# Taking feeds, a first turn and a turn order over into a 1-core RWKV, GLA and short-convolution kernel, with modulation pieces and back-end orders dealt anew

## The reference, cut to what matters

```python
def rwkv7_scan(r, decay, k, v, kk, b, reverse):
    def step(S, inp):
        r_t, w_t, k_t, v_t, kk_t, b_t = inp
        sa = jnp.einsum('bhij,bhj->bhi', S, -kk_t)
        S = (S * w_t[:, :, None, :] + sa[..., None] * b_t[:, :, None, :]
             + v_t[..., None] * k_t[:, :, None, :])
        return S, jnp.einsum('bhij,bhj->bhi', S, r_t)
...
def first_block(x, p, ...):
        z = rms_norm(h, norm_mix_pre[i]) @ w_in[i]
        y = concatenate([rwkv7_mixer(z_rwkv), gla_mixer(z_gla)]) @ w_out[i]
        h = h + rms_norm(y, norm_mix_post[i])
        hn = rms_norm(h, norm_ffn_pre[i])
        f = (silu(hn @ ffn_gate[i]) * (hn @ ffn_up[i])) @ ffn_down[i]
        h = h + rms_norm(f, norm_ffn_post[i])
        e = p[i] @ ple_proj[i]
        gate = jax.nn.sigmoid(h @ ple_gate[i] + ple_gate_b[i])
        h = h + rms_norm(gate * e, norm_ple[i])
...
def second_block(x, c, ada_w, ada_b, ...):
        mod = silu(c) @ ada_w[i] + ada_b[i]
        sh_m, sc_m, g_m, sh_f, sc_f, g_f = jnp.split(mod, 6, axis=-1)
        # modulated norm, short convolution mixer, gated residual; the same around a SwiGLU
```

## Time and the profile before

| | us |
|---|---|
| median of three runs (3123.69 to 3125.21) | 3123.69 |
| profiled execution | 3124.51 |
| its span in the trace | 3122.7 |
| TensorE busy with matmuls | 2912.3 (93%) |
| VectorE busy | 1467.9 (47%) |
| ScalarE busy | 1150.3 (37%) |
| GpSimd busy | 280.8 (9%) |
| stretch from 1044 us on, TensorE busy | 2045 of 2079 |

### The profile page before, as it was taken

How to read it: one execution, slowest core, us unless ns; L and a number is a source line. 1 busy time by engine, 2 the same in 40 slices (tenths; PEclk the granted TensorE clock), 3 DMA queues, 4 the chain that set the end, 5 groups by cost and what they waited for, 6 DMA issues and landing times.

```text
span 3122.7 us, 56580 instructions
## 1 busy us (share of the span) xinstructions
PE 2912.3 (93%) x25024; PEld 2370.8 (76%) x25024; DVE 1467.9 (47%) x2047; ACT 1150.3 (37%) x1891; POOL 280.8 (9%) x318
## 2 busy tenths in 40 slices
PE   6986799688887799999999999999999999999997
PEld 5765666587785488888888887788887888888886
DVE  3668676245454454433343326666436533234323
ACT  5665565222223243322332225533234333242322
POOL 1000023444441100000000000000000000000000
PEclk8987899799998799999999999999999999999998
DMA  4320244311100123222222222222222222223222
...
DMA packets 99541, 273.07 MB, mean 87 GB/s; under 512 B 8224, under 2 KB 35488, under 8 KB 99296
## 3 DMA queue, kind: packets, MB, share of 16 engines
...
## 4 chain that ended last, share of the span: by engine, by line
PE 63%; DVE 2%; ACT 1%; issue 0%; DMA 0%; DVEq 0%; ACTq 0%
PE be_ps L2937 47%; PE be_ps L2958 15%; PE be_ps L2971 1%; DVE be_ring L2719 0%; PE be_ps L2664 0%; PE be_ps L2658 0%; DVE be_total L2677 0%; ACT be_whi L3004 0%; DVE be_raw_r L3111 0%; DVE big L2691 0%; DVE big L2701 0%; ACT big L3010 0%; DMA be_raw<-in_ple_gate 0%; DVE big_r L2729 0%; DVE ext_r L2729 0%
## 5 line engine op out<-in xcount | busy, mean ns | idle before, releaser
L3111 DVE TENSOR_TENSOR be_raw_r<-be_raw,be_whi 128x1024 fp32r<-128x1024 f32 x361 | 442.2, 1225 | 997.3 <-ACT be_whi L3004 996.9
L2937 PE MATMUL be_ps<-ext_r,be_whi 128*128 128x512 f32 x2304 | 714.9, 392 | 13.0 <-PEq L2331 8.6
L3004 ACT CAST be_whi<-be_raw 128x1024 fp32r<-128x1024 f32 x361 | 378.8, 1049 | 898.6 <-DMA be_raw<-in_ffn_down 317.2
L2937 PE MATMUL be_ps<-big_r,be_whi 128*128 128x512 f32 x2048 | 642.2, 394 | 0.8 <-DVE be_raw_r L3111 0.5
L2937 PEld LDWEIGHTS be_ps<-ext_r,be_whi 128*128 128x128 f32 x2304 | 432.9, 189 | 106.5 <-issue 10.6
L2937 PEld LDWEIGHTS be_ps<-big_r,be_whi 128*128 128x128 f32 x2048 | 383.0, 188 | 95.9 <-DVE big_r L2727 1.0
L2937 PE MATMUL be_ps<-ext_r,be_raw_r 128*128 128x512 f32 x1152 | 449.8, 390 | 0.0
L2937 PE MATMUL be_ps<-big_r,be_raw_r 128*128 128x512 f32 x1024 | 408.1, 398 | 0.0
L2958 PE MATMUL be_ps<-ext_r,be_whi 128*128 128x512 f32 x1152 | 354.9, 389 | 0.0
L2937 PEld LDWEIGHTS be_ps<-ext_r,be_raw_r 128*128 128x128 f32 x1152 | 217.1, 188 | 45.5
L2958 PEld LDWEIGHTS be_ps<-ext_r,be_whi 128*128 128x128 f32 x1152 | 216.2, 188 | 45.1
...
## 6 DMA issues: line engine op xcount, KB each, us to landing
be_raw<-in_ffn_gate SPq DMA_DIRECT2D x88, 512.0 KB, 3.5
be_raw<-in_ffn_up SPq DMA_DIRECT2D x88, 512.0 KB, 3.5
be_raw<-in_ffn_down SPq DMA_DIRECT2D x88, 512.0 KB, 3.5
be_raw<-in_conv_in SPq DMA_DIRECT2D x48, 512.0 KB, 3.4
gp_ada<-in_ada POOLq DMA_DIRECT2D x24, 512.0 KB, 3.7
rp_ada<-in_ada POOLq DMA_DIRECT2D x24, 512.0 KB, 3.8
rwkv_prepared<-big SPq DMA_DIRECT2D x16, 512.0 KB, 3.2
be_raw<-in_w_out SPq DMA_DIRECT2D x16, 512.0 KB, 3.5
```

The costliest lines, as they stand in the source:

```text
L2937: mm = pe.matmul(ps[:, bank], part[:, k * P:(k + 1) * P], xs(k), start=(k == 0 and i == 0), stop=(k == KD - 1 and i == 2))
L3004: act.copy(w.hi[:, n % 3], w.raw[:, n % 3]).then_inc(w.hi_ready, 1)
L3111: dve.tensor_tensor(w.lo(n), w.raw[:, n % 3], w.hi[:, n % 3].bitcast(F32), ALU.subtract).then_inc(w.lo_ready, 1)
```

## The change

- **GLA projection.** The pieces per step become 3,3,2,2,2,2,2,3,0,0,3,2 instead of 3,3,2,2,2,2,2,2,0,0,3,3, and the last tile's side products come after its 48 matmuls.
- **RWKV projection.** In step 8 VectorE's reciprocal comes ahead of `accumulate(3)`. SP issues the first four feeds of the mixing at the end of the stage and waits for them. ScalarE ends with a dummy Exp.
- **Mixing, opening.** No feeds for turns 0 and 1; VectorE makes the first alpha and rho in place of GpSimd; the four first score groups get banks 0, 4, 6 and 2 and stand in a row.
- **Mixing, turns.** TensorE's `front_nv(t + 1)` follows `products(0)` instead of `products(1)`; ScalarE's copy of nv comes after both copies of u. A turn's feed is six DMAs of 128 KB instead of two of 384 KB, each waiting for TensorE's marks of four turns before.
- **Back end.** In stage "eg" the groups of steps 2 and 3 take banks 0, 2, 3, 1; norm pieces beside the projections and the last gate are placed at other positions.

The diff, cut to its core:

```diff
@@ -613,7 +613,7 @@
         a_up = sb("aup", [P, 2 * P])
-        modulation = Modulation(core, ctx, "gp", dram_ada, c, mod, 0, (3, 3, 2, 2, 2, 2, 2, 2, 0, 0, 3, 3))
+        modulation = Modulation(core, ctx, "gp", dram_ada, c, mod, 0, (3, 3, 2, 2, 2, 2, 2, 3, 0, 0, 3, 2))
         acc = ctx.enter_context(nc.psum_tensor("gp_acc", [P, 2, T], F32))
@@ -792,7 +792,7 @@
                 for k in range(KD):
-                    if k >= 5 and k - 5 < len(side_products):
+                    if s < n_tiles - 1 and k >= 5 and k - 5 < len(side_products):
                         modulation.product(pe, side_products[k - 5])
@@ -804,6 +804,9 @@
                     decay_sum(n)
+                if s == n_tiles - 1:
+                    for n in side_products:
+                        modulation.product(pe, n)
@@ -1161,6 +1164,22 @@
+def turn_tokens(d, j):
+    n = j if d == 0 else NBLK - 1 - j
+    return slice(n * BLK, (n + 1) * BLK)
...
+def fed_pair(pieces):
+    return pieces.rearrange("p (s d k t) -> p s d k t", s=2, d=2, k=6)
...
+def first_fed(z):
+    return fed_pair(z[:, 12:15].rearrange("p a t -> p (a t)"))
@@ -1185,7 +1204,7 @@
         sem = lambda name: core.sem(f"rp_{name}")
-        first_hi = sem("first_hi")
+        first_hi, fed_early, exp_table = sem("first_hi"), sem("fed_early"), sem("exp_table")
         filled, edged, summed, mixed = (sem(x) for x in ("filled", "edged", "summed", "mixed"))
@@ -1280,6 +1299,17 @@
                     keep_b(s - 10)
+            for i in (0, 1):
+                sp.wait_ge(cum_kept[i], 32)
+                sp.wait_ge(kk_kept[i], 16)
+                sp.wait_ge(b_kept[i], 16)
+            sp.wait_ge(kk_kept[2], 16)
+            sp.wait_ge(*taken("rate", 3, 1))
+            fed = first_fed(z)
+            for t in two:
+                for d in two:
+                    sp.dma_start(fed[:, t, d], prepared[:, 0, 2 * d:2 * d + 6, turn_tokens(d, t)]).then_inc(fed_early, 16)
+            sp.wait_ge(fed_early, 64)
             for i in pairs:
@@ -1383,6 +1413,7 @@
             drain(NZR - 1)
+            act.activation(ka_rest[:, 0:1], cst(core, "ones")[:, 0:1], ACT.Exp).then_inc(exp_table, 1)
@@ -1488,9 +1519,9 @@
                 if s == 8:
-                    accumulate(3)
                     dve.wait_ge(kk_rooted, 1)
                     dve.reciprocal(kk_scale, kk_scale).then_inc(kk_scaled, 1)
+                    accumulate(3)
             modulation.take(dve)
@@ -1676,10 +1707,7 @@
-        def fed_pair(pieces):
-            return pieces.rearrange("p (s d k t) -> p s d k t", s=2, d=2, k=6)
-        fed = (fed_pair(z[:, 12:15].rearrange("p a t -> p (a t)")), fed_pair(sb("fed", [P, 3 * T])[:, :]))
+        fed = (first_fed(z), fed_pair(sb("fed", [P, 3 * T])[:, :]))
@@ -1712,7 +1740,8 @@
         cleared, mod_ready, eyes_ready = core.sem("rw_cleared"), core.sem("rw_mod_ready"), core.sem("rw_eyes_ready")
-        y_taken = core.sem("rw_y_taken")
+        y_taken, first_queried = core.sem("rw_y_taken"), core.sem("rw_first_queried")
+        first_banks = {"beta0": 0, "beta1": 4, "kappa0": 6, "kappa1": 2}
@@ -1738,11 +1767,7 @@
-        def block(d, j):
-            return j if d == 0 else NBLK - 1 - j
-        def tokens(d, j):
-            return slice(block(d, j) * BLK, (block(d, j) + 1) * BLK)
+        tokens = turn_tokens
@@ -1824,12 +1849,13 @@
                 for d in two:
-                    sp.dma_start(fed[t // 2 % 2][:, t % 2, d], prepared[:, g, 2 * d:2 * d + 6, tokens(d, j)]
-                                 ).then_inc(fed_loaded[t % 4], 16)
+                    for k in (0, 2, 4):
+                        if t >= 4:
+                            sp.wait_ge(*pe_made.by(("xx1", "xx2", "xx3", "xx4", "u0", "u1")[3 * d + k // 2], t - 4))
+                        sp.dma_start(fed[t // 2 % 2][:, t % 2, d, k:k + 2],
+                                     prepared[:, g, 2 * d + k:2 * d + k + 2, tokens(d, j)]).then_inc(fed_loaded[t % 4], 16)
             at = CONST["eye64"] * P
             sp.dma_start(masks[:, 0:4].rearrange("p a t -> p (a t)"), dram_const[:, at:at + 4 * P]).then_inc(loaded, 16)
-            feed(0)
-            feed(1)
             sp.dma_start(masks[:, 4:14].rearrange("p a t -> p (a t)"), dram_const[:, at + 4 * P:at + 14 * P]
@@ -1842,7 +1868,8 @@
-                act.wait_ge(fed_loaded[t % 4], t // 4 * 32 + 32)
+                if t >= 2:
+                    act.wait_ge(fed_loaded[t % 4], (t + 2) // 4 * 96)
                 if t:
@@ -1906,8 +1933,8 @@
                              ).then_inc(*act_made(f"u{m}"))
-                    if m == 0 and ahead:
-                        nv_out(t + 1, dve_made.by("rhs1", t))
+                if ahead:
+                    nv_out(t + 1, dve_made.by("rhs1", t))
                 if j < n_turns // 2:
@@ -1986,7 +2013,11 @@
             factors(0, 0, 0)
-            queries(0, 0, 0, 0)
+            pool.wait_ge(cleared, 1)
+            pool.wait_ge(first_queried, 4)
+            pool.wait_ge(*pool_front.by("kappa", 0))
+            pool.sem_inc(*pool_front("alpha"))
+            pool.sem_inc(*pool_front("rho"))
             ends(0)
@@ -2022,13 +2053,13 @@
-            def scores(d, key, par):
+            def scores(d, key, par, bank=F0):
...
                             o = d * 4 * CH + q * P
-                            ins = mm(ps[chunks[c], F0 + h, o:o + P], key[rows_of(h), d, q, chunks[c]],
+                            ins = mm(ps[chunks[c], bank + h, o:o + P], key[rows_of(h), d, q, chunks[c]],
                                      queried[rows_of(h), par, d, q, :, chunks[c]])
@@ -2051,7 +2082,7 @@
                 pe.wait_ge(*pool_front.by("beta_end", t))
-                pe.wait_ge(*dve_front.by("kappa1", t))
+                pe.wait_ge(*dve_front.by("kappa1" if t else "beta0", t))
                 turned(0, lambda d, q: beta_end[:, d, q]).then_inc(*pe_front("beta_tok"))
@@ -2075,13 +2106,17 @@
             pe.wait_ge(loaded, 16)
+            pe.wait_ge(*pool_front.by("beta", 0))
+            pe.wait_ge(first_queried, 4)
             for d in two:
-                front_beta(0, 0, d, None)
+                scores(d, beta, 0, first_banks[f"beta{d}"]).then_inc(*pe_front(f"beta{d}"))
+            pe.wait_ge(*pool_front.by("kappa", 0))
             for d in two:
-                front_kappa(0, 0, d)
+                scores(d, kappa, 0, first_banks[f"kappa{d}"]).then_inc(*pe_front(f"kappa{d}"))
             front_beta_tok(0)
             front_v(0, 0, 0)
+            pe.wait_ge(*dve_front.by("kappa1", 0))
             front_nv(0, 0)
@@ -2200,7 +2235,7 @@
                     products(m)
-                    if m and ahead:
+                    if m == 0 and ahead:
                         front_nv(t + 1, 1 - par)
@@ -2224,6 +2259,12 @@
                 dve.tensor_tensor(gains[:, 3 * half + 2], gate, own[:, 2 * half + 1], ALU.mult).then_inc(mod_ready, 1)
+            dve.wait_ge(*act_exp.by("e_rho", 0))
+            dve.wait_ge(cleared, 1)
+            for d in two:
+                dve.tensor_tensor(by_chunk(alpha[:, 0, d]), by_chunk(kk_of(0, d)), before(d), ALU.mult).then_inc(first_queried, 1)
+                dve.tensor_tensor(by_chunk(rho[:, 0, d]), by_chunk(z[:, 0:2, tokens(d, 0)]), upto(d), ALU.mult
+                                  ).then_inc(first_queried, 1)
             dve.wait_ge(loaded, 16)
@@ -2233,9 +2274,10 @@
                 dst = (by_beta if name[:-1] == "beta" else by_kappa)[:, par, d]
+                bank = F0 if t else first_banks[name]
                 dve.wait_ge(*pe_front.by(name, t))
                 dve.tensor_tensor(dst.rearrange("p h q k t -> p h q (k t)"),
-                                  ps[:, F0:F0 + 2, d * 4 * CH:(d + 1) * 4 * CH].rearrange("p h (q t) -> p h q t", q=2),
+                                  ps[:, bank:bank + 2, d * 4 * CH:(d + 1) * 4 * CH].rearrange("p h (q t) -> p h q t", q=2),
                                   both_scores[:, d].rearrange("p (a b t) -> p a b t", a=1, b=1).to_broadcast([P, 2, 2, P]),
@@ -2506,7 +2548,7 @@
         if stage == "eg" and 2 <= i < 4:
-            return [(a, "dve" if i == 2 and a < 2 else "act") for a in range(4)]
+            return [((0, 2, 3, 1)[a], "dve" if i == 2 and a < 2 else "act") for a in range(4)]
         if stage == "sc":
@@ -2557,10 +2599,11 @@
 BESIDE_PROJECTION = dict(sum_y=0.5, spread_y=1.5, scale=[1, 2, 2, 3, 3, 4, 4, 5], h_add=[2, 2, 3, 3, 4, 4, 5, 5],
-                         sq_h=[2, 3, 3, 4, 4, 5, 5, 5], sum_h=6, spread_h=6.5, norm=[6, 6, 6, 7, 7, 7, 7, 7],
-                         lo=[6, 6, 7, 7, 7, 7, 7, 7])
+                         sq_h=[2, 3, 3, 4, 4, 5, 5, 5], sum_h=6, spread_h=6.5, norm=[6, 6, 6, 6, 7, 7, 7, 7],
+                         lo=[6, 6, 6, 7, 7, 7, 7, 7])
+BESIDE_LAST_GATE = dict(BESIDE_PROJECTION, norm=[6, 6, 6, 6, 6, 7, 7, 7], lo=[6, 6, 6, 6, 7, 7, 7, 7])
 AFTER_PROJECTION = Plan(sq_y=[m - 7 for m in range(KD)], **BESIDE_PROJECTION)
```

(2 more changed lines are left out.)

## The result

| | us |
|---|---|
| before, median of 4 runs beside the changed kernel (3123.69 to 3132.62) | 3124.45 |
| changed, median of 4 runs (3090.01 to 3099.02) | 3093.01 |
| changed, profiled execution (its span 3088.2) | 3090.01 |
| forecast | 3083.3 (3073 to 3092) |

The ratio of the two is 0.9896, 95% interval 0.9873 to 0.9919; the forecast was 3083.3 / 3123.7 = 0.9871. Applied to the 3123.7 that the forecast started from, the ratio gives 3091.2, just under the top of its range; the median itself lies 1.0 above it. The direction and most of the mechanisms hold, but a gain of some 32 us was measured where 40 were forecast. Times on either side spread more than the three runs of before suggested: in 38 further runs beside the experiments the kernel before took 3121.8 to 3135.1, 3129.2 at the median, so the gain may be some 4 us larger than 32.

What follows compares the result with a forecast made beforehand. From 1044 us on matmuls bind TensorE, so gains come from the front or single stalls. Terms −0.1, −6.2, −12.6, −18.0, 0, −3.5 and 0 sum to −40.4 against 3124.5: 3084.1, less 0.8 gives 3083.3 us; range 3073 to 3092.

Steps and rivals of the forecast that it cites:

- GLA projection, −0.1: Redealt pieces in the GLA projection: −0.1 us, since VectorE's accumulates end the stage; bounds −5.9 and +1.7.
- The replay of that loss: GLA projection tile by tile: TensorE idles 0.8, 0.5, 2.0 and 2.9 us, tile 12 ends near 214.0, not 211.5.
- Reciprocal, −6.2: RWKV projection: reciprocal first removes 2.81 us idle and 3.4 of clock fall; −6.2 us, bound −2.8.
- Opening, −12.6: Opening of the mixing: first scores 9.6 us earlier, groups back to back; −12.6 us, between −11.7 and −13.6.
- under 10: Sign for the mixing's opening: first scores under 10 us after the last projection matmul.
- Turn order, −18.0: 15 of 16 mixing turns: to_state(1) 1.26 us sooner, to_state(0) loses 0.05; −1.2 a turn, −18.0 us, bounds −13.5 to −19.5.
- its slower rival: Mixing turns: earlier nv group and more feed DMAs break up TensorE's issue, clock falls every turn; 64 us, total 3148; chance 3%.
- signs of being wrong: Nv copies block something on ScalarE, feeds land late, or the clock falls in the turns or GLA tiles.
- Feeds, 0: Mixing turns, two DMAs become six: zero; bounds −4.3, or a microsecond or two lost to more issues.
- Embedding, −3.5, gate 0: Back end: bank order removes 1.80 us wait and 1.7 of clock loss, −3.5 us; last gate's plan 0.
- its bound of −3.2: Last gate step in the back end: −3.2 us if the clock holds after the idle shrinks to 2.4 us.
- The rival of the opening at −11.7: Mixing's opening: VectorE and GpSimd shut each other out, gain only −11.7 us; total given as 3085.0; chance 12%.

Runs made afterwards that it cites:

- warm: Changed kernel plus unread matmuls: 20 of 128x512 behind the RWKV projection's last tile, 80 of 64x64 at the mixing's start; median 3115.2 us, ratio 0.9952 to before.
- warm16: Changed kernel plus unread matmuls: 20 of 128x512 behind the RWKV projection's last tile, 16 of 64x64 at the mixing's start; median 3092.9 us, ratio 0.9883 to before.
- no_feeds: Changed kernel without the feeds of turns 4 to 15, which reuse the values of turns 0 to 3; median 3087.1 us, ratio 0.9875 to before.
- hold: Changed kernel with to_state(1) made to wait for ScalarE's copy of the next turn's nv; median 3094.7 us, ratio 0.9889 to before.

## Why the prediction was right in direction and 8 us too good

1. **GLA projection, −0.1.** Right: −0.4 in the profile, 0 to −1 over all profiles. The step that made it right is that VectorE ends the stage, so that what TensorE loses to the third piece's lateness doesn't count. The replay of that loss was right by luck: it had 6.2 us of idle, the trace shows 3.6 (0.74, 0.19, 1.81 and 0.84), and tile 12 ended near 214.0 of the time of before all the same, because the clock fell in between.
2. **Reciprocal, −6.2.** Right in both halves: −6.1 behind the first tile (−6.7 and −6.3 with it), and −5.0 (−2.2 to −8.1) alone.
3. **Opening, −12.6.** Right, −13.3 here and −13.7 in five other profiles (20.5 us). Two errors cancel in part: the first scores came 8.7 us sooner and not 9.6 (10.1 us behind the last projection matmul, where "under 10" was the sign), and the groups behind them gave 4.6 and not 4.0. The conflict of VectorE and GpSimd is real: 0.96 and 0.28 us on two pairs of keys. The Trainium skill, "SBUF — State Buffer", section "two separate sides", says that a VectorE operation with two SBUF inputs and a GpSimd operation that reads SBUF lock a shared port pair, and that the one that starts first holds it for its whole length. By it I had the sum at −11.7; the trace agrees that the two cost each other time, but here VectorE's products took their usual 0.42 us and only GpSimd's pair beside them grew longer, by less than the 1.7 us that I had counted.
4. **Turn order, −18.0.** The step that failed in size. "−1.26" at `to_state(1)` was right: from one state addition of a turn to its second 3.54 us pass instead of 4.81. The first half paid more than the 0.05 forecast: its state addition comes 1.92 us after products(0) instead of 1.82. So the undisturbed turns 4 and 14 went from 23.4 to 22.3 and 22.4, which makes −16 to −17 over 15. Over turns 1 to 15 the profile shows −12.7; ten profiles with the moved group, all feeds and no added wait took 346.4 to 358.9 us there, 350.2 on average, so −9.4 against the 359.6 and 359.8 of the old order; and the runs of the order alone gave −10.3 in total. What takes the rest back are stalls of TensorE's issue, 5.3 to 7.8 us in twelve profiles with the moved group against 2.7 and 3.5 in two without, and falls of the clock after some of them (0.93 over turn 2). The forecast named this chain as its slower rival, by feeds and group alike, and gave it 3% at 64 us; it came true in small, by the group and not by the feeds. One of the prediction's signs of being wrong, a fall of the clock in the turns, did show.
5. **Feeds, 0.** Right: 0.9890 against 0.9896.
6. **Embedding, −3.5, gate 0.** The banks gave −3.7 in the profile; the plan gave 1 to 2.5 us instead of nothing, because the idle was cut in two pieces (0.88 and 2.23) behind which the clock held, as it did in five of nine profiles. The forecast had this as its bound of −3.2.
7. **Base.** The sum was made against a profile with 2.7 us of stalls whose time, 3124.5, lies in the lower part of what 38 further runs gave. The start (+1.4) is a difference between executions: the other kernels, with the same code ahead of it, began the first GLA matmul at 49.6 to 51.0. Of the finish (+2.2) that is not shown: it took 74.6 to 75.8 us in the four kernels with the opening and back end of before and 75.1 to 77.2 in the ten others, so about 1 us may stay, and its cause is open.
8. **Two slips in the sums.** The rival of the opening at −11.7 lies 0.9 above the forecast, which is 3084.2 and not 3085.0; and the terms named for the top of the range add up to about 3093, not 3092.

**What the stalls wait for** can be read from the DMA packets in the traces. In the mixing of the 14 profiles TensorE has 103 issue stalls of 0.35 us or more. All 103 end 1.2 to 1.7 us after a 16 KB instruction packet of q8 has come to its end, a stretch that makes up about an eighth of the time between two packets. The packet had come late as a rule: 4.8 us at the median after the start of the one before it, where 3.9 is usual. So the stalls are waits for late instruction packets, as far as traces can tell; no run delayed a packet by itself. They stand at the same few instructions in many kernels (mx-xt, x25, in turn 2 of nine of the twelve). The kernels warm and warm16, with added matmuls ahead, stall elsewhere, both at the same three instructions (rw_by_kappa,rw_v_tok x9 in turn 8, rw_mx,rw_xt x10 in turn 9, rw_x,rw_by_beta x9 in turn 13), though they differ by 64 matmuls; those are 256 records of matmuls and weight loads, just about one packet. So the place in the packet matters.

**Open** is why the moved group makes packets come late more often. Neither the feeds (no_feeds) nor the half microsecond of pause (hold) changes it.
